# One subtraction of 128x2048 for the low parts of a weight slot, in place of two of 128x1024, in a two-layer encoder trunk

## What is computed

```python
D_MODEL = 2048; SEQ = 256; D_FF = 4 * D_MODEL

def short_conv_mixer(xn, w_in, conv_w, w_out):
    b_gate, c_gate, h = jnp.split(xn @ w_in, 3, axis=-1)
    u = c_gate * h
    conv = lax.conv_general_dilated(u, conv_w[:, None, :], window_strides=(1,), padding=[(1, 1)], ...)
    return (b_gate * conv) @ w_out

def sq_relu_mlp(xn, w_up, w_down):
    return jnp.square(jax.nn.relu(xn @ w_up)) @ w_down

    for l in range(DEPTH):
        hn = rms_norm(h, mix_norm_g[l])
        h = h + mixer(hn, ...)
        hn = rms_norm(h, mlp_norm_g[l])
        h = h + sq_relu_mlp(hn, mlp_w_up[l], mlp_w_down[l])
    return rms_norm(h, final_norm_g)
```

## Time and profile before

| what | value |
|---|---|
| median of 3 runs | 2250.88 us (2250.88 to 2250.92) |
| the profiled execution | 2250.66 us, its span 2248.9 us |
| mean granted TensorE clock | 0.999 of full speed |
| TensorE matmul, busy | 2232.2 us, 99%, 10291 matmuls |
| VectorE, busy | 1831.8 us, 81% |
| ScalarE, busy | 1338.3 us, 60% |
| the chain that ended last | PE 92%, DVE 5%, ACT 1% |
| HBM read | 422.79 MB, 189 GB/s over the span |

### The profile page before, as it was taken

How to read it: one execution, slowest core, us unless ns; L and a number is a source line. 1 busy time by engine, 2 the same in 40 slices (tenths; PEclk the granted TensorE clock), 3 DMA queues, 4 the chain that set the end, 5 groups by cost and what they waited for, 6 DMA issues and landing times.

```text
span 2248.9 us, 28920 instructions
## 1 busy us (share of the span) xinstructions
PE 2232.2 (99%) x10291; PEld 1838.4 (82%) x10291; DVE 1831.8 (81%) x1952; ACT 1338.3 (60%) x1740; POOL 289.5 (13%) x415
## 2 busy tenths in 40 slices
PE   9999999999999999999999999999999999999998
PEld 7888888888788888888888888888888888888887
DVE  5777778866888888888876989886888888888885
ACT  6555555537666666666656566565665665665664
POOL 4444555520000000000000000000000000000000
PEclk9999999999999999999999999999999999999999
DMA  9555555556678678679657878757687787786755
GB/s 266 169 155 162 149 162 156 150 169 223 207 243 263 206 243 266 202 243 270 200 168 242 238 229 240 231 157 252 186 283 199 232 282 201 231 285 200 227 175 176
DMA packets 326401, 479.89 MB, mean 213 GB/s; under 512 B 13930, under 2 KB 145811, under 8 KB 319635
## 3 DMA queue, kind: packets, MB, share of 16 engines
q1 hardware_dynamic: 318322, 423.88, 57.3%
q0 software_dynamic: 7344, 53.48, 12.8%
q10 hardware_dynamic: 624, 1.07, 0.1%
HBM read 422.79 MB, written 2.10 MB: 189 GB/s over the span
## 4 chain that ended last, share of the span: by engine, by line
PE 92%; DVE 5%; ACT 1%; issue 1%; SPq 0%; DMA 0%; POOLq 0%; POOL 0%; ACTq 0%; DVEq 0%
PE pair L471 20%; PE pair L473 20%; PE pair L480 20%; PE m L1165 9%; PE m L1157 9%; PE m L1160 9%; DVE w_lo L572 2%; DVE raw L1946 1%; PE m L1218 1%; PE m L993 1%; PE m L1057 1%; ACT w_hi L568 0%; DVE w_lo L452 0%; PE m L924 0%; PE m L1007 0%
## 5 line engine op out<-in xcount | busy, mean ns | idle before, releaser
L568 ACT ACTIVATE w_hi<-raw 128x1024 fp32r<-128x1024 f32 x796 | 808.6, 1054 | 614.9 <-DVE raw L1946 311.2
L572 DVE TENSOR_TENSOR w_lo<-raw,w_hi 128x1024 fp32r<-128x1024 f32 x796 | 940.2, 1220 | 227.8 <-ACT w_hi L568 224.6
L471 PE MATMUL pair<-w_hi,yT_hi 128*128 128x512 f32 x1264 | 499.6, 395 | 0.0
L473 PE MATMUL pair<-w_hi,yT_lo 128*128 128x512 f32 x1264 | 492.7, 390 | 0.0
L452 DVE TENSOR_TENSOR w_lo<-raw,w_hi 128x1024 fp32r<-128x1024 f32 x208 | 256.2, 1253 | 138.0 <-ACT w_hi L441 136.9
L441 ACT ACTIVATE w_hi<-raw 128x1024 fp32r<-128x1024 f32 x208 | 218.1, 1058 | 246.1 <-PE pair L480 241.3
L480 PE MATMUL pair<-w_lo,yT_hi 128*128 128x512 f32 x1264 | 338.2, 389 | 0.0
L471 PE MATMUL pair<-w_hi,xT_hi 128*128 128x512 f32 x832 | 331.1, 398 | 0.0
L473 PE MATMUL pair<-w_hi,xT_lo 128*128 128x512 f32 x832 | 324.5, 390 | 0.0
L480 PEld LDWEIGHTS pair<-w_lo,yT_hi 128*128 128x128 f32 x1264 | 237.3, 188 | 50.0
L471 PEld LDWEIGHTS pair<-w_hi,yT_hi 128*128 128x128 f32 x1264 | 237.5, 188 | 48.3 <-DVE yT_lo L1840 0.5
(11 more groups left out here) (188 smaller groups left out, 2299.3 us busy)
## 6 DMA issues: line engine op xcount, KB each, us to landing
raw<-in_mlp_w_up SPq DMA_DIRECT2D x128, 1024.0 KB, 7.1
raw<-in_mlp_w_down SPq DMA_DIRECT2D x256, 512.0 KB, 6.6
raw<-in_ab_w_in SPq DMA_DIRECT2D x256, 256.0 KB, 4.0
raw<-raw POOLq DMA_DIRECT2D x51, 1024.0 KB, 8.6
raw<-in_conv_w_in SPq DMA_DIRECT2D x32, 1024.0 KB, 6.6
raw<-in_ab_w_out SPq DMA_DIRECT2D x64, 256.0 KB, 4.5
raw<-in_conv_w_in SPq DMA_DIRECT2D x32, 512.0 KB, 5.3
raw<-in_conv_w_out SPq DMA_DIRECT2D x32, 512.0 KB, 5.4
```

Source lines behind the costliest of these rows:

```text
L471: nc.tensor.matmul(dst[:, tt], at(hi, kt, tt), w_hi[:, ring, q], start=begin, stop=False)
L473: nc.tensor.matmul(dst[:, tt], at(lo, kt, tt), w_hi[:, ring, q], start=False, stop=False)
L568: nc.scalar.activation(w_hi[:, entry % HALVES], src, ACT.Copy).then_inc(hi_ready, 1)
L572: nc.vector.tensor_tensor(w_lo[:, entry % HALVES], src, w_hi[:, entry % HALVES].bitcast(F32), ALU.subtract).then_inc(lo_ready, 1)
```

## The change

VectorE gets a second helper, `lo_of_slot`, which waits until both halves of a slot have their `w_hi`, subtracts them in one instruction of 128x2048, and then raises `lo_ready` by 2. `split` calls it for X and D slots when both halves are asked for at once. P slots, the calls for one half and all that comes before the first MLP stay as they are.

```diff
+        def lo_of_slot(eng, slot, src):
+
+            at = 2 * slot % HALVES
+            eng.wait_ge(hi_ready, 2 * slot + 2)
+            nc.vector.tensor_tensor(w_lo[:, at:at + 2].rearrange("p a b n -> p (a b) n"), src,
+                                    w_hi[:, at:at + 2].rearrange("p a b n -> p (a b) n").bitcast(F32),
+                                    ALU.subtract).then_inc(lo_ready, 2)
...
                     r, name, second = unit_at(st, slot)
-                    if name[0] == "X":
+                    if name[0] == "X" and ks == (0, 1):
+                        lo_of_slot(dve, slot, raw[:, raw_slot(slot)])
+                    elif name[0] == "X":
                         split_lo(dve, slot, 0, 0, ks)
+                    elif name[0] == "D" and ks == (0, 1):
+                        n = d_at(st, r, int(name[1]), 0) % 4
+                        lo_of_slot(dve, slot, raw_d[:, n:n + 2].rearrange("p a b n -> p (a b) n"))
                     elif name[0] == "D":
                         for k in ks:
                             lo_of(dve, 2 * slot + k, raw_d[:, d_at(st, r, int(name[1]), k) % 4])
```

## The result

The changed kernel takes 2266.11 us (median of 4 runs, 2265.51 to 2267.15) against 2250.90 for the kernel before (4 runs, 2250.88 to 2251.22): ratio 1.0068, 95% interval [1.0053, 1.0083]. That is 15.2 us slower. 2259.4 was predicted, with a range up to 2263.5: the direction was right, the size was too small. The profiled execution is the slowest of the four, 2267.15 us with a span of 2265.4, so 16.5 us longer in span than the one of before.

A forecast was written before the change was run, and what follows sets the result against it. TensorE, busy 99% of the span, was taken as the bound. Steady MLP rounds 4.4, first rounds 0.4, conv 2.35, X slots 0.3 and end 1.05 sum to 8.5 us on 2250.88: 2259.4 us, range 2254 to 2263.5.

The forecast's parts named there:

- What a merged slot does: X and D slots: VectorE saves 0.07 us, the first half is ready 1.06 later, VectorE waits for the second w_hi.
- towards 20: Sign to look for: TensorE's waits on w_lo grow from 14.0 us towards 20, with new ones at D5 and D2.
- TensorE goes on at 727.29 where it wanted to at 727.11: +0.18: D5 in steady MLP rounds: merged low ready late after D4's delay, TensorE 0.18 us later, plus 0.14 for the restart.
- P6, "+0.05": Steady MLP rounds: D0's 0.19 us delay less 0.14 saved at D1 and D2 makes TensorE 0.05 later at P6.
- D2's wait of 0.23: Steady MLP rounds: new TensorE wait of 0.23 us at D2, taken out of the later wait at P6.
- The other X slots have microseconds of slack: X slots other than X3: slack hides their delays, so no cost; without it each would cost up to 1.06 us.
- effect 3: Merged slots: VectorE stands still where it comes before the second half's w_hi, and all behind it in its queue moves back.
- as have the last rounds' D slots: Last rounds' D slots: microseconds of slack hide their delays, no cost; without it each would cost up to 1.06 us.
- Conv stage, 2.35: Conv rounds 1 to 3: 0.65, 1.5 and 0.2 us from late lows, sum 2.35.
- The end, 1.05: Last block's third group of matmuls: TensorE waits 0.95 us for D7's merged low, 1.05 with a restart.
- Loads, 0: D slots' load buffers come free together, the first at least 1.06 us later; counted as 0 because of cover.
- Rival A: Not slower: VectorE's saving reaches TensorE at P6, 2248.0 to 2249.9 us; chance 0.04 within 0.2%, 0.03 faster.

The follow-up runs named there:

- The wait alone: Against the kernel before: the 169 slots keep two subtractions of 128x1024, one signal each, both behind the second w_hi's wait; 2258.82 us against 2250.45.
- the late signal alone: Against the kernel before: two subtractions of 128x1024, each behind its own w_hi, but lo_ready goes up by 2 only at the second; 2251.67 us.
- the run with the end apart: Against the change: D0 to D7 of the last MLP's last round in two subtractions of 128x1024 again; 2264.53 us against 2250.73 before.
- The run with D1, D2, D3, D6 and D7: Against the kernel before: only these slots merged, in the seven whole rounds of both MLPs (70 slots); 2248.86 us against 2250.55.

## Why the prediction was right in direction and short in size

- **What a merged slot does** (less work, later first half, a wait): right. 169 merged instructions of 2.29 us, VectorE 11.3 us less busy (12 to 27 said). The wait alone and the late signal alone carry 8.4 and 1.2 us, and D5, where they meet, brings the rest. TensorE's waits for lows before weight loads grew from 14.0 us to 33.0, and not "towards 20".
- **"TensorE goes on at 727.29 where it wanted to at 727.11: +0.18"**: the mechanism was right, the place was right, the term was mis-sized: 0.35, and 0.12 for the restart (0.14 said). The working put 0.03 us between ScalarE's end and VectorE's start, from lows that carry their wait themselves. The merged low raises `lo_ready` by 2 and has its wait in an instruction of its own, which takes 0.10, and D4 and D5 stand in one chain, so the 0.07 enters twice. 13 rounds at 0.47 and one at 0.83 (D5's low 0.37 later still, cause open) make 6.9 in place of 4.5. The trace of before had three lows that start at 0.10, all with such a wait ahead of them, so the 0.03 should have been a bound. A difference of 0.18 between sums of 2 to 17 us can't be better than such terms.
- **P6, "+0.05"**: 0.11 measured in the 12 steady rounds, 0.7 us more in all. The same 0.07 at D0's start is the likely reason; it was not run by itself. In the two first rounds 0.13 and 0.12 came back there, 0.14 said. D2's wait of 0.23 that "comes out of the later wait at P6" is right: 0.28, with its restart, and given back.
- **"The other X slots have microseconds of slack"**: this step failed. It looked at each slot's own w_lo, and not at what is queued behind it on VectorE, although effect 3 says just that. X6's wait moved a hidden_lo that a turn of TensorE needs: 0.9 us in each MLP, 1.8 of the missing 6.7. X3 cost 0.14, 0.1 said.
- **"as have the last rounds' D slots"**: failed in the same way in the conv stage's round 4, where a turn waits for VectorE behind a merged D0: 0.43 (seen in the timelines, not run apart), and in the MLPs' last rounds where a load comes late (0.94 in the change's profile).
- **Conv stage, 2.35**: 2.74, of which 0.34 is again a turn (P5 in round 2) that the sum did not have; the rest of round 2 gave 1.3 against 1.5, round 1 gave 0.82 and round 3 0.29 against 0.65 and 0.2. That the rest comes out at 2.4 is in part luck, since round 1 was a value picked between two bounds.
- **The end, 1.05**: about 1.2 in the timelines; the run with the end apart agrees within its noise.
- **Loads, 0**: right for the rounds. Where D follows D it is not quite: the stops of 0.24 to 1.06 us in five profiles need a late load. The waits for w_down grew from 8.5 to 14.2 us in the change's profile. In the median at most the 0.4 us between 14.8 and 15.2 can be theirs.
- **Rival A** (VectorE's saving reaches TensorE) is false for the change and true for a part of it: ahead of P6 the saved time does reach it. The run with D1, D2, D3, D6 and D7 is 1.7 us faster, and the change gets about as much back there and loses more elsewhere.
- **Range**: it reached up for 0.1 us at each D5 and for conv round 2, which make 1.9 of its 4.1 us, and "for places that I took as covered", which leaves 2.2 for them. By the timelines those places were worth 2.7 (X6, X3's excess, round 4 and the turn in round 2), D5's excess 2.4 and P6's 0.7.

## What to carry to other kernels

Merging two instructions saved 0.07 us each time here, and puts the second one's wait in front of the first: look up, slot by slot, whether the later operand is ready when the engine comes, and merge only there. A slot is not covered because its own result is early; ask for each added wait what is the next thing in that engine's queue that somebody waits for. Look, too, at where the merged instruction's own wait stands: with its signal raised by 2 it started 0.07 later behind ScalarE. Two delays that each fit into the same slack must be tested together, and a forecast that rests on a small difference of long chains needs a range as wide as the uncertain start-up times on it, multiplied by the number of rounds.

## What the runs showed of the hardware

A subtraction on VectorE that waits for ScalarE's result starts 0.03 us after it when the wait is part of the instruction (3612 cases), and 0.10 after it when the wait stands in an instruction of its own (76 cases at 128x1024, 624 at 128x2048, eight of all these at 0.46 or 0.47). A signal that is raised by 2 brought the second form in each of its cases (all 169 in the change), a wait for a second semaphore too (three cases in each profile). In a full queue a subtraction starts 0.08 us before the end of the one ahead, at either size and in either form of the wait. After a stop at D2, at D5 and at the lows of a P slot, TensorE's next matmuls took 0.11 to 0.14 us longer than in an unbroken row, also where the stop was only 0.07 long (D2 in the run with D2 merged); at the turns it was 0.03 to 0.06. A stop moved ahead of another one cost nothing here, because the second restart fell out with its wait. Between profiled executions TensorE's work behind the load of x, at 17 us, started up to 0.9 us apart, which is the size of several of the effects measured here; timelines compared slot by slot told them apart where medians could not.
